# Seven products instead of eight for the x, B and C projections of a Mamba-2 layer, computed ahead of the scans

## The reference, cut to what matters

```python
proj = u @ w_in                              # z 2048, x 2048, B 512, C 512, dt 32 columns
xbc = silu(causal_depthwise_conv(xbc, conv_w, conv_b))      # 4 taps, on x, B and C
dt = softplus(dt_raw + dt_bias); A = -exp(A_log)
y = ssd_chunked(x, dt, A, B, C) + x * D      # chunks of 128 tokens, 4 groups of 8 heads
y = y * silu(z); y = y * rsqrt(mean(y * y per group) + eps) * norm_w
return y @ w_out
```

## Time and profile before

| | |
|---|---|
| median of 3 runs | 2308.45 us (2308.16 to 2309.12) |
| span of the profiled execution | 2307.1 us |
| TensorE busy | 2286.2 us, 99% |
| VectorE, ACT, POOL busy | 1261.0, 1056.0, 1197.2 us |
| DMA | 247.92 MB, 107 GB/s over the span |

### The profile page before, as it was taken

The page is one execution under the profiler, slowest core; times in us unless marked ns, Lnnn a source line. Parts: engine busy times, 40 slices in busy tenths (PEclk is TensorE's granted clock), DMA queues, the critical chain, the costliest instruction groups (busy, mean ns, idle before and its releaser), DMA issues.

```text
span 2307.1 us, 29399 instructions
## 1 busy us (share of the span) xinstructions
PE 2286.2 (99%) x10830; PEld 1870.6 (81%) x10830; DVE 1261.0 (55%) x1660; ACT 1056.0 (46%) x1901; POOL 1197.2 (52%) x842
## 2 busy tenths in 40 slices
PE   8999999999999999999999999999999999999998
PEld 6877878888888888788888888888878888888887
DVE  7356663333336777557258247338763333336777
ACT  4046543333333446475256247238543333333445
POOL 3224288777774654223224223314388777774654
PEclk9999999999999999999999999999999999999999
DMA  5100322323228743121222212113222323227754
GB/s 162 48 26 19 119 87 87 119 87 123 88 106 295 243 149 112 57 92 47 65 61 68 73 41 88 49 52 101 101 81 94 119 87 119 87 101 282 256 148 158
DMA packets 166964, 247.92 MB, mean 107 GB/s; under 512 B 18464, under 2 KB 111532, under 8 KB 164268
## 3 DMA queue, kind: packets, MB, share of 16 engines
q1 hardware_dynamic: 162204, 233.99, 30.7%
q10 hardware_dynamic: 4624, 12.06, 1.4%
HBM read 192.93 MB, written 53.08 MB: 107 GB/s over the span
## 4 chain that ended last, share of the span: by engine, by line
PE 93%; DVE 2%; POOL 2%; issue 1%; DMA 1%; ACT 1%; SPq 0%; ACTq 0%; POOLq 0%; DVEq 0%
PE ps L1752 32%; PE ps L1478 12%; PE ps L1480 12%; PE ps L1479 12%; PE ps L1838 5%; PE ps L1846 5%; PE ps L1842 5%; PE ps L2038 1%; PE ps L2030 1%; POOL p_lo L774 1%; PE ps L2023 1%; POOL p_val L800 1%; PE ps L1501 1%; PE ps L1675 1%; PE ps L1708 1%
## 5 line engine op out<-in xcount | busy, mean ns | idle before, releaser
L749 POOL TENSOR_TENSOR w_lo<-w_raw,w_hi 128x1024 fp32r<-128x1024 f32 x74 | 176.5, 2389 | 376.3 <-ACT w_hi L927 329.7
L853 POOL TENSOR_TENSOR s_lo<-s_val,s_hi 128x512 fp32r<-128x512 f32 x154 | 234.3, 1523 | 202.3 <-ACT s_hi L1256 202.2
L2314 DVE TENSOR_TENSOR xres<-ps,xres 128x512 f32<-128x512 f32 x132 | 90.5, 688 | 409.5 <-PE ps L1752 409.5
L1478 PE MATMUL ps<-xn_hi,w_hi 128*128 128x512 f32 x784 | 310.2, 396 | 0.0
L1479 PE MATMUL ps<-xn_lo,w_hi 128*128 128x512 f32 x784 | 305.5, 390 | 0.0
L1480 PE MATMUL ps<-xn_hi,w_lo 128*128 128x512 f32 x784 | 305.3, 389 | 0.0
L774 POOL TENSOR_TENSOR p_lo<-p_val,p_hi 128x512 fp32r<-128x512 f32 x176 | 238.4, 1363 | 44.8 <-ACT p_hi L1068 33.7
L1068 ACT ACTIVATE p_hi<-p_val 128x512 fp32r<-128x512 f32 x176 | 111.1, 632 | 310.6 <-POOL p_val L800 310.6
L1752 PE MATMUL ps<-xn_hi,p_hi 128*128 128x512 f32 x704 | 189.0, 390 | 3.1 <-ACT xres L1171 3.1
L1752 PE MATMUL ps<-xn_lo,p_hi 128*128 128x512 f32 x704 | 188.2, 389 | 0.0
L1752 PE MATMUL ps<-xn_hi,p_lo 128*128 128x512 f32 x704 | 188.2, 389 | 0.0
(11 more groups left out here) (293 smaller groups left out, 4922.8 us busy)
## 6 DMA issues: line engine op xcount, KB each, us to landing
s_val<-hidden SPq DMA_DIRECT2D x154, 256.0 KB, 2.8
hidden<-xres SPq DMA_DIRECT2D x20, 1792.0 KB, 6.5
wv_g<-in_w_gate SPq DMA_DIRECT2D x22, 1024.0 KB, 5.1
wv_u<-in_w_up SPq DMA_DIRECT2D x20, 1024.0 KB, 5.1
w_raw<-in_ssd_w_in SPq DMA_DIRECT2D x40, 512.0 KB, 3.9
d_val<-in_w_down SPq DMA_DIRECT2D x70, 256.0 KB, 3.9
rows_v<-in_w_down SPq DMA_DIRECT2D x64, 256.0 KB, 3.7
mdec<-decay_sums SPq DMA_DIRECT2D x32, 512.0 KB, 4.0
```

The costliest lines, as they stand in the source:

```text
L749: pool.tensor_tensor(w_lo[piece.slot][:, :], raw[piece.raw][:, :], f(w_hi[piece.slot][:, :]), ALU.subtract).then_inc(lo_done, 1)
L853: pool.tensor_tensor(s_lo[i][:, :], s_val[i][:, :], f(s_hi[i][:, :]), ALU.subtract)\
L1478: pe.matmul(dst, l_hi, r_hi, start=first, stop=False, skip_group_check=reopened)
```

## The change

The x, B and C projections leave the groups. A new stage `q_stage` stands between `ffn(0)` and the first group on every engine:

- B and C of group 0 are computed plainly (`bc_sums`, 96 matmuls), while tiles 4 to 7 are transposed (`turn_T`) and the token sums T1 to T4 are formed (on ACT `turn_first` and `turn_hi`, on VectorE `turn_sums`, `turn_rests`, `turn_lo`, on POOL `turn_lo1`, `turn_t4`, `turn_lo3`). Their split weights are loaded and split during the down slices.
- The other 22 column blocks form 11 pairs of blocks, in the slots "g" and "u" of six steps p (the sixth has only "g"), each with seven products as in the feed-forward. First tap, taps and SiLU (`tap0`, `taps`, `row_silu`) follow each block; the rows are stored to DRAM (`conv_rows`, `store_row`) from four buffers in the place of tiles 4 to 7 of `xres`, and each group loads its six rows in two halves of the tokens (`load_rows`).
- The residual x is parked in DRAM and comes back during the first scan (`x_back`); the first output of group 0 waits for it.
- Step-size rows, folds and decay sums come in the last step. Their buffers lie in the place of `xres`.
- The loop over groups is written out. A group has 8 pieces (4 of z, 4 of `w_out`) instead of 14; seven of them are split inside the scan instead of five. Gate units: in group 0, 0 and 1 around product M4g and the decay sums, 2 to 4 ahead of the first chunk, one after each of chunks 0 to 2; in groups 1 to 3, 0 and 1 ahead of the first chunk, two after each of chunks 0 to 4. `gc`, a group's copy of the constants, goes.

The core of the diff:

```diff
-        HI_AFTER_CHUNK = {0: (9,), 1: (10,), 3: (11,), 4: (12,), 6: (13,)}
-        Z_AFTER_CHUNK = {-1: (0, 1), 0: (4,), 1: (5, 6), 2: (7,), 3: (8, 9), 4: (10, 11), 5: (12,), 6: (13,),
-                         7: (14, 15)}
+        HI_AFTER_CHUNK = {0: (1, 2), 1: (3,), 2: (4,), 3: (5,), 4: (6,), 6: (7,)}
+        Z_BEFORE = {False: (0, 1), True: (2, 3, 4)}
+        Z_AFTER_CHUNK = {False: {0: (2, 3), 1: (4, 5), 2: (6, 7), 3: (8, 9), 4: (10, 11), 5: (12,), 6: (13,), 7: (14, 15)},
+                         True: {0: (5,), 1: (6,), 2: (7,), 3: (8, 9), 4: (10, 11), 5: (12,), 6: (13,), 7: (14, 15)}}
+        DECAY_AFTER_PIECE = {3: (2,), 4: (3,), 5: (4,), 6: (5,), 7: (6, 7)}
...
+        Q_BLOCKS = [(0, "x0"), (0, "x1")] + [(g, n) for g in range(1, G) for n in ("bc", "x0", "x1")]
...
SP, in each group:
+                    load_piece(0)
+                    load_piece(1)
+                    sp.wait_ge(ydiag_full, t.count("chunk", -1))
+                    load_decay(0)
+                    load_piece(2)
...
+                    sp.wait_ge(out_full, t.count("out", -NT))
+                    load_rows(g, 0)
+                    sp.wait_ge(out_full, t.count("out"))
+                    load_decay(1)
+                    load_rows(g, 1)
+                for k in range(3, GP):
+                    load_piece(k)
                     for c in DECAY_AFTER_PIECE.get(k, ()):
                         load_decay(c)
+                    if g == 0 and k == 5:
+                        store_row(row_at(NQ - 1, "g", 1))
+                        store_row(row_at(NQ - 1, "g", 2))
+                        sp.wait_ge(gc_ready, 1)
+                        for i in range(4):
+                            sp.wait_ge(row_stored[i], 16 * ((len(ROWS) - 1 - i) // 4 + 1))
+                        for tt in range(NT):
+                            sp.dma_start(xres[:, tt, :], parked_x[tt]).then_inc(x_back, 16)
...
TensorE, q_stage:
+                bc_sums(0, 0, 0)
+                turn_T(0)
+                bc_sums(0, 0, 1, range(4))
+                turn_T(1)
+                bc_sums(0, 0, 1, range(4, NK))
+                bc_sums(0, 0, 2)
...
+                bc_sums(1, 0, 0)
+                turn_T(2)
+                bc_sums(1, 0, 1)
+                bc_sums(1, 0, 2)
+                turn_T(3)
...
+                pe.wait_ge(q_turn_hi, q_turn_hi_order.count(0, "B22", 3))
+                bc_sums(0, 1, 0)
...
+                bc_sums(0, 1, 2).then_inc(bc_full, 1)
+                bc_sums(1, 1, 2).then_inc(bc_full, 1)
+                for mn in Q_FIRST:
+                    q_product(0, mn)
+                for p in range(1, NQ - 1):
+                    q_product(p, "M1g")
+                    q_product(p - 1, "M4u")
+                    q_product(p, "M2g")
+                    q_product(p, "M5g")
+                    q_product(p, "M6g")
+                    q_product(p, "M3g")
+                    q_product(p, "M7g")
+                    q_product(p, "M1u")
+                    q_product(p, "M4g")
+                    q_product(p, "M2u")
+                    q_product(p, "M5u")
+                    q_product(p, "M6u")
+                    q_product(p, "M3u")
+                    q_product(p, "M7u")
...
+                q_product(p, "M6g")
+                pe.wait_ge(wdt_split, 3)
+                pe.wait_ge(taps_done, row_at(p - 1, "u", 2) + 1)
+                dt_rows(0)
+                dt_rows(1).then_inc(dt_rows_full, 1)
+                q_product(p, "M3g")
+                folds()
+                q_product(p, "M7g")
...
TensorE, ahead of the chunks of a group:
+                if g == 0:
+                    pe.wait_ge(taps_done, row_at(NQ - 2, "u", 1) + 1)
+                    z_half(0)
+                    q_product(NQ - 1, "M4g")
+                    z_half(1)
+                    decay_sum_rows()
+                    pe.wait_ge(taps_done, row_at(NQ - 1, "g", 1) + 1)
+                    token_major(0)
+                    pe.wait_ge(taps_done, row_at(NQ - 1, "g", 2) + 1)
+                    for i in Z_BEFORE[True]:
+                        z_half(i)
+                else:
+                    pe.wait_ge(out_added, t.count("out", -1))
+                    z_half(0)
+                    pe.wait_ge(rms_rooted, t.count("rms"))
+                    token_major(0)
+                    pe.wait_ge(out_added, t.count("out"))
+                    for i in Z_BEFORE[False][1:]:
+                        z_half(i)
...
VectorE, in the last step:
+                step_sizes(lambda: q_block(p, "22", "g"), lambda: taps(row_at(p, "g", 1)))
+                taps(row_at(p, "g", 2))
```

More of the change, by code:

```diff
@@ new lines, in trunk @@
+        Q_NEXT = [(0, n) for n in ("M2g", "M5g", "M6g", "M3g", "M7g", "M1u", "M4g", "M2u", "M5u", "M6u", "M3u", "M7u")]
+        Q_LAST = [(NQ - 1, n) for n in ("M2g", "M5g", "M6g", "M3g", "M7g")]
+        q_order = Order([(0, n) for n in Q_FIRST] + [(1, "M1g"), (0, "M4u")]
+                        + [(p + s, n) for p in range(1, NQ - 1) for s, n in Q_NEXT + [(1, "M1g"), (0, "M4u")]]
+                        + Q_LAST + [(NQ - 1, "M4g")])
+        q_split = ([(0, n) for n in ("M5g", "M6g", "M3g", "M1g", "M7g", "M2g", "M1u", "M2u", "M4g", "M5u", "M6u", "M3u", "M7u")]
+                   + [(1, "M1g"), (0, "M4u")] + [(1, n) for n in ("M2g", "M5g", "M6g", "M3g", "M7g")]
+                   + [(p + s, n) for p in range(1, NQ - 1)
+                      for s, n in ((0, "M1u"), (0, "M4g"), (0, "M2u"), (0, "M5u"), (0, "M6u"), (0, "M3u"), (0, "M7u"),
+                                   (1, "M1g"), (0, "M4u"), (1, "M2g"), (1, "M5g"), (1, "M6g"), (1, "M3g"), (1, "M7g"))]
+                   + [(NQ - 1, "M4g")])
@@ L683, in load_decay @@
                         sp.wait_ge(ydiag_full, t.count("chunk", c - 1))
[L684 to L690, removed]
-                    else:
[L692 to L699, removed]
+                    sp.dma_start(mdec[c % 2][:, :, :].rearrange("p h l -> p (h l)"),
+                                 decay_sums[g:g + 1, c, :].to_broadcast([P, HG * P])).then_inc(decay_loaded[c % 2], 16)
@@ L702, in ssd_group @@
                 t.add("chunk", NT)
-                t.add("silu", NCB)
-            t = Tally(chunk=0, silu=0)
-            with sp.Fori(0, G - 1) as g:
-                t.enter(g, chunk=NT, silu=NCB)
+                t.add("out", 2 * NT)
+            t = Tally(chunk=0, out=2 * NT)
+            for g in range(G):
                 ssd_group(g)
-                t.leave(G - 1)
-            ssd_group(G - 1)
             ffn(1)
@@ L896, in ssd_group @@
                     ins.then_inc(sq_summed, 1)
+                if not last:
+                    lo(piece(GP))
                 t.add("sq", 2 * BG)
@@ L900, in ssd_group @@
                 t.add("carry", NT - 1)
-            with pool.Fori(0, G - 1) as g:
-                t.enter(g, chunk=NT, half=2 * NT, carry=NT - 1, sq=2 * BG, added=2 * (BG - 2))
-                ssd_group(g)
-                t.leave(G - 1)
-            ssd_group(G - 1)
+            for g in range(G):
+                ssd_group(g, g == G - 1)
             ffn(1)
@@ L1422, in ssd_group @@
                     split(b, 0)
-                if not last:
-                    hi(piece(GP))
                 root(0)
@@ L1432, in ssd_group @@
                     root(1)
+                    hi(piece(GP))
+                    table(ACT.Exp)
+                    t.add("out", 2 * NT)
                 t.add("z", 2 * BG)
[L1434 to L1455 removed]
+                return root
+            for g in range(G):
+                root = ssd_group(g, g == G - 1)
             ffn(1, lambda: root(1))
@@ L1970, in ssd_group @@
+            ffn(0)
+            q_stage()
             def ssd_group(g, last=False):
                 piece = in_group(g)
-                assert t.n["unit"] % 2 == 1
-                for k in range(3, NCB):
-                    project(piece(k))
-                t.add("conv", NCB)
                 def z_half(i):
@@ L2084, in ssd_group @@
                 t.add("rms", 2)
-                if not last:
-                    for k in range(3):
-                        project(piece(GP + k))
-            with pe.Fori(0, G - 1) as g:
-                t.enter(g, unit=NCB, conv=NCB, z=2 * BG, chunk=NT, half=2 * NT, out=2 * NT, carry=NT - 1, rms=2)
-                ssd_group(g)
-                t.leave(G - 1)
-            ssd_group(G - 1, True)
+            for g in range(G):
+                ssd_group(g, g == G - 1)
             ffn(1)
```

1034 lines of the change are left out of this document (745 added, 289 removed).

## The result

The changed kernel takes **2345.2 us** (median; 2343.6 to 2347.2) against 2308.8 for the kernel before on the same chip: ratio 1.0157, 95% interval 1.0143 to 1.0171. The forecast was 2297, faster; the kernel is slower, and outside the range.

What follows compares the result with a forecast made beforehand. TensorE, busy 99% of the span, was taken to bound the kernel. -29.9 + 6.5 + 5.9 + 6.0 = -11.5 on 2307.1 gave 2295.6; with the median 1.35 above the span, 2297 us, range 2280 to 2311.

Steps and rivals of the forecast that it cites:

- What is removed: x, B and C projections: 132 fewer matmuls at 0.2268 us each take 29.9 us off TensorE, bounds 29.5 to 30.3.
- Inside the product stage: Product pairs of x, B, C: the new taps and SiLUs finish in time, costing 0, bounds 0 to 11 us.
- wrong if pairs exceed 38.5: Stated sign of error for the new stage: product pairs were to be 38.1 us long, not above 38.5.
- M6's copy: In each product pair, ScalarE's copy for product M6, behind a SiLU: ready after 3.8 us, needed after 5.4.
- The entry: Start of the new stage: TensorE waits on transposes, copies, sums and taps, costing 6.5 us, bounds 1 and 12.
- The exit: From the new stage into the first scan: TensorE waits for the last rows' taps, 5.9 us, bounds 2 and 10.
- Group 0: First scan, chunk 5: its decay load waits behind the residual's eight loads, costing 6.0 us, bounds 0 and 13.
- Groups 1 to 3: Later groups: row loads and decays are covered, costing 0; a group takes 118 us instead of 183.
- (c): Rival: the scans turn from TensorE to ACT, 24 us, giving a slower kernel at 2321; chance 0.09.
- (d): Rival: taps keep POOL out, pairs run 7.1 us over, +39, giving a slower kernel at 2336; chance 0.04.
- Rival (b): The new stage's pairs lengthen by the 2 us bound, +11, giving 2308, no change; chance 0.13.

Runs made afterwards that it cites:

- a_same: The changed kernel with the removed tile `gc` kept, unused, so every shared buffer stands at its byte in the kernel before: 2321.3 us.
- a_same_u: a_same with the load of the second pair's `u` weights issued ahead of a row store in SyncE's queue, not behind it: 2315.7 us.
- a_four: a_three with ScalarE's three copies of the last transposed tile ahead of two splits of the tile before's sums: 2303.1 us.
- a_aligned: The changed kernel with eight unused floats per partition behind the small constants, so the shared buffers start at byte 178688: 2334.9 us.
- a_three: a_same with earlier second-pair `u` load, later raw B and C weight loads and splits, and residual loads behind the first scan's last loads: 2306.0 us.
- a_same_x: a_same with the residual stream's eight loads behind the first scan's last weight piece and last decays: 2312.5 us.

## Why the prediction was wrong

**What is removed (-29.9): the count right, the pitch not.** 132 matmuls went. The prediction took 0.2268 us for every matmul of both kernels and gave the term "narrow" bounds, since "at both ends of this term stands the same pitch". That is the step that failed. The matmuls that stayed got dearer wherever `comb` or `t` meets a weight: 23.9 us by a_same. Where they lie: 7.0 us before the first down slice (699.6 before, 706.6 after), 7.7 in the second layer's products (367.3 against 375.0), 0.8 in each of the new stage's pairs, some 1.2 in each of groups 1 to 3. No part of the prediction looked at what removing a tile does to the address of the tiles behind it.

**Inside the product stage (0, bounds 0 to 11; "wrong if pairs exceed 38.5"): wrong in the changed kernel.** The pairs are 38.88 us apart (ScalarE's first copy of each pair), but 38.08 in a_same: the length is the pitch again, and from the third pair on the argument on the engines' queues holds. At the second pair SyncE's queue, which that paragraph did not lay out, held a load back behind a row store: 5.6 us by the medians of a_same_u, 3.7 to 4.5 by the traces. The place that the paragraph called the tightest, M6's copy, cost 1.55 there, and nothing in the other pairs. Both are inside the bound of 11, where the sum had nothing.

**The entry (+6.5): mechanism right, 2.7 too small.** In a_same_u, start to start less the pitch, waits of 0.94, 0.45, 4.76 and 1.49 us against 0.9, 0, 4.3 and 1.3, and 1.6 more in passes at a lower clock behind the 4.76, a term that the sum did not have. a_four shows that it is ScalarE's order, as the prediction laid it out. Its lower bound rests on a misread row: the longest wait at a feed-forward entry before is not the 1.44 of the earlier trace rows but 1.61, at the first one.

**The exit (+5.9): mechanism right, 3 too small.** The two waits on the taps are 2.9 and 4.4 (1.3 and 4.6 forecast); the rest is clock again, 1.5 in a_same_u. In the profiled execution of the changed kernel the clock takes 3.0 there.

**Group 0 (+6.0): mechanism right, a second late item missed.** The decay landed 16.8 us after the first of the eight loads was issued (16.6 forecast), its mask was ready after 22.5 (22.8 forecast), and alone it would have cost 5.9. But the weight piece and its place on GpSimd's queue, which the paragraph named and did not follow, held TensorE up earlier: the wait at chunk 5 is 4.6, with 1.6 of passes at the lower clock behind it. Taking both away was worth 8.7.
The Trainium skill ("DMA: Bandwidth & Descriptors", Queues, rings and completion order) has each DMA engine take a queue's descriptors in ring order; the trace agrees in this case: the piece issued behind the eight loads landed after 10.70 us, later than all eight.

**Not in the sum: the down-projection.** Two loads of B's and C's weights into its busiest stretch: 3.0 us of waits in a_same, 1.6 in the medians.

**Groups 1 to 3 (0, a group of 118): right.** 118.1 in a_same_u and 119.3 in the changed kernel, the difference being pitch. Rivals (c) and (d) did not come: chunks stand 9.2 apart, and pairs of 38.08 leave no room for a GpSimd kept out. Rival (b) had the sign of the pairs but another cause.

**The sum.** From 2297 to 2345.2 are 48: place 23.9, queue 5.6, entry 2.7, exit 3, residual 2.7, down-projection 1.6, the copy's wait in the second pair 1.6: 41. Of the 7 left, 2 are the median, which lies 3.4 above the profiled span of 2341.8 and not 1.35, and 1.7 stand at the second layer's entry, where the wait that was 1.4 in the earlier trace rows is longer:

```profile
1745.42 1.15 PE L2159 MATMUL ps<-xn_hi,p_hi 128*128 128x512 f32 x4 [2.67 <-ACT xres L1443]
```

In a_same and most of its descendants this wait is 3.0 to 3.3, with low-clock passes behind it, 3.2 us in all; but in a_same_u it is 1.5, and in a_aligned 1.1. Part of it is a matter of the single execution: at the first layer's entry, up to which all kernels of a_same's family run the same instructions, the wait is 3.0 in a_same and a_three and 1.4 to 1.6 in the others. Why is open: it was not tried. The last 3 are not accounted for; they are within what the medians scatter. The shares are measured by taking each away, mostly from a_same; that they also add up in the changed kernel itself is not shown.

## What to carry to other kernels

A tile that is added or removed moves every tile behind it: before pricing an edit at the old pitch, compare the byte distance, modulo 256, of the operands that meet in the hot matmuls, and pad it back to zero. When a stage moves, lay out every in-order queue it touches, SyncE's too; here a load behind a row store cost some 4 to 6 us, where the whole entry cost 9. When one late item is found, ask what else was late behind it. And behind each exposed wait of 3 us or more, look for passes at the lower clock: here they cost from nothing to 3.0 us.

## What the runs showed of the hardware

- **Operand distance.** With 128x512 fp32r matmuls on this chip four matmuls take 0.907 us when moving and stationary operand lie a multiple of 256 bytes apart, and 0.93 to 0.94 at distances of 32, 96, 128 and 192 (modulo 256): 2 to 4%. Moving all tiles together by 128 bytes changed nothing (b_all, ratio 0.9992). The passes that follow on an undisturbed operand are partly slow too: in the changed kernel `xn_hi` by `q_hi` took 0.92. Which hardware does this, and whether it goes for other shapes and types, no run here tells.
- **The clock behind a wait.** In a_same's first feed-forward entry a wait of 3.00 us is followed by passes that start 1.84 and 1.42 apart instead of 0.91, half speed at first (a granted clock of 0.50: 1.2 instead of 2.4 GHz), 1.4 us in all; behind the wait of 1.61 us at the same place in the kernel before they start 1.00 and 0.93 apart, at a granted clock of 1.00. In the changed kernel the granted clock of 940 to 950, which holds most of the wait of 4.60 us, is 0.78; from 948.4 to 952.4, behind it, 0.50.

```profile
333.27 2.05 PE L2160 MATMUL ps<-xn_hi,p_hi 128*128 128x512 f32 x4 [3.00 <-ACT xres L1444]
335.11 1.58 PE L2160 MATMUL ps<-xn_lo,p_hi 128*128 128x512 f32 x4
336.53 1.09 PE L2160 MATMUL ps<-xn_hi,p_lo 128*128 128x512 f32 x4
```

- **The loss is not fixed by the wait.** The same wait of 3.29 us, in the second pair, is followed by no slow pass in a_same (the first two lines) and by 2.8 us of loss in a_same_x (the last two):

```profile
1010.10 1.15 PE L2160 MATMUL ps<-xn_hi,q_hi 128*128 128x512 f32 x4 [3.29 <-ACT q_tmp22g L1627]
1011.09 1.07 PE L2160 MATMUL ps<-xn_lo,q_hi 128*128 128x512 f32 x4
...
1006.80 2.04 PE L2161 MATMUL ps<-xn_hi,q_hi 128*128 128x512 f32 x4 [3.29 <-ACT q_tmp22g L1628]
1008.64 1.91 PE L2161 MATMUL ps<-xn_lo,q_hi 128*128 128x512 f32 x4
```

Behind the wait of 4.60 at the entry the loss was 1.5 to 2.8 us in the kernels that have it, behind the exit's second wait 1.5 to 3.0. No single wait of 1.8 us or less was followed by the lower clock in any of the traces, from 320 us on.
